# Toeplitz products in four column tiles, pooling bands built at the start, rows of y ahead of gate rows in a trunk kernel

## The chip, the cores and the metric

The kernel is one launch on one core of a Trainium2 chip. Its time is in device microseconds (us), taken from the start to the end of the program on that core; lower is better. A core has five engines that run their own instruction streams and wait for each other on semaphores: TensorE (PE in the profile; PEld is its weight load), VectorE (DVE), ScalarE (ACT), GpSimd (POOL) and SyncE (SP, which here only issues transfers). ScalarE issues some transfers too. Matmul results land in PSUM, 8 banks of 128 x 512 float32.

## The reference, cut to what matters

Two layers over 512 tokens of width 1024, float32. Each sub-layer is an RMS norm with shift, scale and gate made from a conditioning vector `c` (adaLN), a mixer or an MLP, and a gated residual. The change lies in the first mixer, `_ab_mixer`, and in the adaLN products beside it:

```python
def _modulate(x, c, g, w, b):
    m = (c @ w + b)[:, None, :]
    shift, scale, gate = jnp.split(m, 3, axis=-1)
    h = _rmsnorm(x, g) * (1.0 + scale) + shift
    return h, 1.0 + gate

def _ab_mixer(h, ...):
    proj = h @ w_in                         # 1024 -> 512 (ua) + 512 (ub)
    ya = _pool_mixer(ua, pool_w, pool_scale)  # trailing means over 2, 4, 8, 16 tokens, minus identity
    yb = _s5_mixer(ub, ...)                 # 32 groups of 16 channels, 64 complex states each
    return jnp.concatenate([ya, yb], axis=-1) @ w_out
# in _s5_mixer: y = Re(C h) + D u;  y = gelu(y);  y = y * sigmoid(y @ w_glu + b_glu)
```

## The kernel before

Every large product is done as three float32r products (high by high, high by low, low by high), so each weight slot of 1024 x 256 is loaded by SyncE into `w_raw`, rounded by ScalarE to `w_hi` (`prep` on ScalarE, L751) and subtracted by VectorE to `w_lo` (`prep` on VectorE, L1283). TensorE then makes two tiles of 128 x 512 a slot, 24 products each (`tile`, `first_tiles`). Two buffers of each kind alternate, so ScalarE may round slot n only when TensorE has finished slot n-2.

The order of each engine's instructions is written by hand; nothing schedules them. What stands around the change, in order of time:

- **Start.** VectorE computes the parameters of the SSM (`sm`, `pw_re`, `bz`, `f_re`, `f_im`). TensorE multiplies `c` with the first adaLN columns (`ada_pair`) and sums them to columns by products with ones (`ada_columns`, 128x1). `first_scales` on VectorE must be done before the second `ada_columns`, and `first_shifts` follows that. `modulate(0)` then gives `h_hi`, `h_lo`, and the input projection `AB_IN` (four slots) starts.
- **SSM.** TensorE transposes `f` to `e_re`, `e_im` (what a run of eight tokens puts into the states), multiplies the inputs with it (`injections`) and VectorE scans over the 64 runs in two halves (`chain`). The part inside a run is a Toeplitz matrix per group: its 16 x 128 first rows `kr` come from 32 products of `bd` (32 columns of weights) with `g_re` and `g_ni`, four `skip_d` products add the diagonal. ScalarE copies `kr` out of PSUM, and 16 transfers (8 of SyncE at L569, 8 of ScalarE at L873) shift it into `toep`. `half_outputs` multiplies `toep` with the inputs and adds the states' part, for 16 groups at a time.
- **Exchange of y.** ScalarE applies GELU into `y_run`. Eight transfers a half write it to memory by rows (L584 on SyncE, L890 on ScalarE), two read it back by channels into `y_t` (L588). ScalarE and VectorE split it into `yg_hi` and `yg_lo`, and TensorE makes the GLU product from these.
- **Pooling.** `v_tok` is the product of `ua` with the pooling weights, copied by ScalarE. The trailing means are products with four banded matrices, `band(g)` and `first_band(g)` (the first 16 columns), which `make_band` builds on VectorE from `steps_off`. TensorE waits for them with `bands`.
- **Gates.** The remaining adaLN columns are six units (2 to 7) of eight steps each. A step adds one block of 128 rows times its entry of `c` on VectorE (`ada_step`, L1108 for the first of a unit, L1111 for the others, 128x512 in units 2 and 3, 128x768 in 4 to 7). The rows come from memory: sixteen in `ada_mid`, then 32 through eight homes, three in `ada_ring` and five in `ada_more`, each refilled when its step is done (`more_ada`, L534). When a unit's eight steps are done, TensorE sums it to columns (`ada_sums`, products with ones, alternating between PSUM banks 6 and 7), and VectorE adds the bias (`ada_collect`, L1240). `ada_sums` of unit 3 waits until unit 2 is collected.
- **Output projection** `AB_OUT`, four slots. Between two tiles of each slot TensorE makes the `ada_sums` of one unit (4 to 7), and VectorE adds the gated residual (L1431). GpSimd adds up the squares of the new x (L675). The norm of the first MLP begins with TensorE's sums of `sumsq`.

## Time and profile before

| | |
|---|---|
| median of 3 runs | 1289.25 us (1288.05 to 1290.51) |
| profiled execution | 1290.38 us, span 1288.6 us |
| busy: TensorE, VectorE, ScalarE, GpSimd | 96%, 59%, 35%, 7% of the span |
| mean granted clock of TensorE | 0.984 |
| ScalarE rounds a weight slot (L751) | mean 1895 ns |
| VectorE's low half of a slot (L1283) | mean 2320 ns |
| VectorE's gated residual (L1431) | mean 750 ns |
| one product of 128x512, start to start, 24 in a tile | 0.23 us |

A busy share is a mean over stages. TensorE's idle time is short and lies in a few places, so the waits and the timeline tell more than the shares. The granted clock is a share of TensorE's full speed: 1.00 is 2.4 GHz and 0.50 is 1.2 GHz. A float32 product leaves two records in the trace, a float32r product leaves one, so "x32" of float32 products are 16 of them. A number such as 0.39 us for a product is its own latency; the next starts 0.23 us after it.

### The profile page before, as it was taken

The numbers are of one execution on the slowest core, as the hardware profiler recorded it, in microseconds if no ns is written. First come the engines' busy times: TensorE is split into PE (matmuls) and PEld (weight loads), VectorE is DVE, ScalarE is ACT, GpSimd is POOL, SyncE is SP. The second block draws the span as 40 slices with busy tenths as digits, with TensorE's granted clock in tenths as the row PEclk, the third lists the DMA queues.
The fourth block names the chain that finished last, engine by engine and source line by source line (L and its number), as shares of the span: only waits on it lengthen the run. The fifth ranks groups of instructions, "written<-read, shape, count | busy, mean of one in ns | idle before, by whom it ended". The sixth has DMA issues, their size and how long they took to land.

```text
span 1288.6 us, 16165 instructions
## 1 busy us (share of the span) xinstructions
PE 1241.1 (96%) x6192; PEld 1004.8 (78%) x6192; DVE 761.0 (59%) x1041; ACT 448.7 (35%) x611; POOL 94.8 (7%) x128
## 2 busy tenths in 40 slices
PE   6999599999999999999999998999999999999999
PEld 3788588788888888888779885567788888888887
DVE  7898777754654645655468957864643443443432
ACT  5442412421422312323443247862432231331321
POOL 0010012000000000051000001114100000000022
PEclk9999799999999999999999998999999999999999
DMA  9558755544445444431223220003143223223311
GB/s 322 187 116 261 244 192 197 172 160 154 146 168 171 171 163 131 171 112 58 83 70 122 82 89 1 1 1 98 33 131 98 76 98 92 92 98 98 98 65 65
DMA packets 132686, 157.40 MB, mean 122 GB/s; under 512 B 19784, under 2 KB 113152, under 8 KB 132608
## 3 DMA queue, kind: packets, MB, share of 16 engines
q1 hardware_dynamic: 125328, 153.82, 36.4%
q10 hardware_dynamic: 7312, 2.96, 1.1%
q8 instruction: 30, 0.49, 0.2%
q14 instruction: 16, 0.13, 0.0%
...
## 4 chain that ended last, share of the span: by engine, by line
PE 84%; DVE 9%; DMA 3%; ACT 2%; issue 1%; SPq 1%; ACTq 0%; POOL 0%; DVEq 0%
PE psum L1646 83%; PE psum L1650 2%; DVE ada_acc_b L1111 1%; DVE work L1294 1%; DMA ada_first<-in_ada_w 1%; DVE w_lo L1283 1%; DVE h_lo L1304 1%; DVE ada_acc L1111 1%; DMA raw_bn<-in_ssm_b_im 1%; DMA y_scratch<-y_run 1%; ACT pT L1034 1%; SPq L534 0%; DVE s_t L1082 0%; DVE rstd L1111 0%; DVE s_im L1082 0%
## 5 line engine op out<-in xcount | busy, mean ns | idle before, releaser
L1646 PE MATMUL psum<-h_hi,w_hi 128*128 128x512 f32 (+1 forms) x872 | 343.1, 393 | 3.4 <-DVE w_lo L1283 3.3
L1646 PE MATMUL psum<-h_lo,w_hi 128*128 128x512 f32 (+1 forms) x872 | 340.5, 390 | 0.0
L1646 PE MATMUL psum<-h_hi,w_lo 128*128 128x512 f32 (+1 forms) x872 | 340.4, 390 | 0.0
L751 ACT ACTIVATE w_hi<-w_raw 128x2048 fp32r<-128x2048 f32 x92 | 174.3, 1895 | 285.6 <-PE psum L1646 285.0
L1283 DVE TENSOR_TENSOR w_lo<-w_raw,w_hi 128x2048 fp32r<-128x2048 f32 x92 | 213.4, 2320 | 100.2 <-ACT w_hi L751 99.7
L1646 PE MATMUL psum<-a_hi,w_hi 128*128 128x512 f32 x512 | 202.4, 395 | 0.0
L1646 PE MATMUL psum<-a_hi,w_lo 128*128 128x512 f32 x512 | 202.2, 395 | 0.0
L1646 PE MATMUL psum<-a_lo,w_hi 128*128 128x512 f32 x512 | 202.1, 395 | 0.0
L1646 PEld LDWEIGHTS psum<-h_hi,w_hi 128*128 128x128 f32 (+1 forms) x872 | 164.0, 188 | 42.6 <-issue 7.2
L1646 PEld LDWEIGHTS psum<-h_hi,w_lo 128*128 128x128 f32 (+1 forms) x872 | 163.9, 188 | 35.0
L1646 PEld LDWEIGHTS psum<-h_lo,w_hi 128*128 128x128 f32 (+1 forms) x872 | 163.9, 188 | 33.8
L1431 DVE SCALAR_TENSOR_TENSOR xT<-psum,mods,xT 128x512 f32<-128x512 f32 x80 | 59.4, 750 | 187.6 <-PE psum L1646 187.5
L1477 DVE TENSOR_TENSOR work<-work 128x512 f32<-128x512 f32 x64 | 44.2, 691 | 127.4 <-ACT work L945 126.6
L1646 PEld LDWEIGHTS psum<-a_hi,w_lo 128*128 128x128 f32 x512 | 96.3, 188 | 23.0
L1646 PEld LDWEIGHTS psum<-a_lo,w_hi 128*128 128x128 f32 x512 | 96.3, 188 | 22.8
L1646 PEld LDWEIGHTS psum<-a_hi,w_hi 128*128 128x128 f32 x512 | 96.3, 188 | 22.7
L945 ACT ACTIVATE work<-psum 128x512 f32<-128x512 f32 x64 | 38.2, 598 | 212.3 <-PE psum L1646 212.3
L1467 DVE SCALAR_TENSOR_TENSOR ada_acc<-ada_l_ring,pb,ada_acc 128x768 f32<-128x768 f32 x56 | 60.0, 1072 | 1.1
L663 POOL TENSOR_TENSOR sumsq<-xT 128x512 f32<-128x512 f32 x3 | 3.1, 1041 | 682.2 <-DVE xT L1431 682.2
L1481 DVE TENSOR_TENSOR a_lo<-work,a_hi 128x512 fp32r<-128x512 f32 x64 | 44.3, 693 | 2.6
L948 ACT ACTIVATE a_hi<-work 128x512 fp32r<-128x512 f32 x64 | 40.5, 633 | 2.0
L1646 PE MATMUL psum<-w_hi,h_hi 128*128 128x256 f32 x128 | 36.4, 284 | 0.0
...
## 6 DMA issues: line engine op xcount, KB each, us to landing
...
```

The source lines that it names most:

```text
L751: act.activation(w_hi[n % 2][:, :, 0:w], raw[n % 2][:, :, 0:w], ACT.Copy).then_inc(hi_ready, 1)
L945: act.activation(work[t % 2][:, 0:L], bank[(t0 + t) % 4], ACT.Relu)\
L948: act.activation(a_hi[:, t, :], work[t % 2][:, 0:L], ACT.Square)\
L1034: act.activation(pT[:, 0:i + 1, i * P:(i + 1) * P], bank[n % 2][:, 0:(i + 1) * P].rearrange("p (j q) -> p j q", q=P), ACT.Copy).then_inc(t ...
L1111: ins = dve.scalar_tensor_tensor(out=acc[:, 0:w], in0=row, scalar=pb[:, k:k + 1], in1=acc[:, 0:w], op0=ALU.mult, op1=ALU.add)
L1283: dve.tensor_tensor(w_lo[n % 2][:, :, 0:w], raw[n % 2][:, :, 0:w], w_hi[n % 2][:, :, 0:w].bitcast(F32), SB).then_inc(lo_ready, 1)
L1431: dve.scalar_tensor_tensor(out=xT[:, k, :], in0=bank[t % 4], scalar=mods[:, a, 16 + k:17 + k], in1=xT[:, k, :], op0=M, op1=A).then_inc(dve ...
L1467: ins = dve.scalar_tensor_tensor(out=ada_acc[:, :], in0=src, scalar=pb[:, k:k + 1], in1=ada_acc[:, :], op0=M, op1=A)
L1477: dve.tensor_tensor(work[2][:, 0:L], work[t % 2][:, 0:L], work[t % 2][:, 0:L], M)\
L1481: dve.tensor_tensor(a_lo[:, t, :], work[2][:, 0:L], a_hi[:, t, :].bitcast(F32), SB)\
L1646: return nc.tensor.matmul(o, lhsT, rhs, start=start, stop=stop, **kw)
L1650: return nc.tensor.transpose(o, in_, ident[0:n, 0:n])
```

## The change

There are four parts.

1. **Toeplitz products.** `kr_part(q)` is quarter q of the partitions of PSUM bank 0. Groups t, t+1, t+2, t+3 go to the four quarters (four column tiles), where before all went to the first 32 partitions of banks 0 and 1 in turn. ScalarE copies quarters 0 and 1, VectorE quarters 2 and 3 inside `chain(0)`.
2. **Bands.** `make_band` runs at the start: band 0 before VectorE's wait for `setup_act`, bands 1 to 3 between `f_im` and `first_scales`. A band is five operations where it was seven, and it lies in `ada_acc`. GpSimd makes `steps_off` without waiting for `h_ready`.
3. **Transfers.** SyncE issues the second `w_out` slot and the first three gate rows behind the exchange of y.
4. **Gate steps and sums.** `ada_sums` of unit u waits for the collecting of unit u-2 (the last user of its bank) and not u-1. The steps are spread anew: 20 before the output projection where there were 25, and 28 in it.

```diff
--- before.py
+++ after.py
@@ -189,14 +189,14 @@
 
     def band(g):
 
-        return work[g // 2][:, g % 2 * (BAND + PAD):g % 2 * (BAND + PAD) + BAND]
+        return ada_acc[:, g * (BAND + PAD):g * (BAND + PAD) + BAND]
 
     def first_band(g):
 
-        return work[g // 2][:, g % 2 * (BAND + PAD) + BAND:(g % 2 + 1) * (BAND + PAD)]
-
-    steps_off = work[0][:, 2 * (BAND + PAD):2 * (BAND + PAD) + BAND]
-    band_tmp = work[1][:, 2 * (BAND + PAD):2 * (BAND + PAD) + BAND]
+        return ada_acc[:, g * (BAND + PAD) + BAND:(g + 1) * (BAND + PAD)]
+
+    steps_off = work[3][:, 0:BAND]
+    band_tmp = work[3][:, BAND:2 * BAND]
 
     at = [e_at]
     s_re = lay(at, "s_re", [P, GT, NRUN])
@@ -488,6 +488,9 @@
         return y_dram.rearrange("(g c) t -> c g t", c=C)[
             :, half * GT:(half + 1) * GT, i * NRUN:(i + 1) * NRUN]
 
+    def kr_part(q):
+        return bank[0][2 * C * q:2 * C * (q + 1), :]
+
     block = nc.Block()
     block.__enter__()
 
@@ -562,7 +565,7 @@
               .then_inc(u_in, 16)
         load(AB_OUT, slots[AB_OUT])
 
-        sp.wait_ge(mats_out, 12)
+        sp.wait_ge(kr_ready, 4)
         sp.wait_ge(toep_zero, 1)
         for m in range(1, RUN, 2):
             for g2 in range(2):
@@ -576,8 +579,6 @@
             sp.dma_start(ada_mid[:, 2 * j:2 * j + 2, :],
                          ada_w[0, a, j % 4 * 2 * P:(j % 4 + 1) * 2 * P, c0:c0 + w].rearrange("(r p) n -> p r n", p=P))\
               .then_inc(ada_mid_in[j], 16)
-        load(AB_OUT + 1, slots[AB_OUT + 1])
-        more_ada(3)
         for half in range(2):
             sp.wait_ge(y_copied, 2 * half + 2)
             for i in range(1, RUN, 2):
@@ -586,11 +587,13 @@
             sp.wait_ge(y_out_s[half], 16 * RUN)
             for ct in (2 * half, 2 * half + 1):
                 sp.dma_start(y_t[:, ct, :], y_dram[ct * P:(ct + 1) * P, :]).then_inc(y_in[half], 16)
-        more_ada(6)
+        more_ada(3)
+        load(AB_OUT + 1, slots[AB_OUT + 1])
+        more_ada(5)
         load(AB_OUT + 2, slots[AB_OUT + 2])
         more_ada(8)
         load(AB_OUT + 3, slots[AB_OUT + 3])
-        more_ada(15)
+        more_ada(16)
         assert ada_next[0] == 2 * ADA_STEPS - ADA_EARLY
         sp.wait_ge(cat_ready, 8)
 
@@ -645,7 +648,6 @@
         own(pool.iota(rot_c[:, 0, :].bitcast(I32), pattern=[[1, NRUN]], base=0, channel_multiplier=0))
         settle()
         pool.tensor_copy(run_no[:, :], rot_c[:, 0, :].bitcast(I32)).then_inc(consts, 1)
-        pool.wait_ge(h_ready, 8)
         own(pool.iota(band_tmp.bitcast(I32), pattern=[[1, BAND]], base=0, channel_multiplier=-1))
         settle()
         pool.tensor_copy(steps_off, band_tmp.bitcast(I32)).then_inc(steps_ready, 1)
@@ -861,12 +863,11 @@
         for r in range(2):
             copy_tile(first_tile[AB_IN + 2] + r, ua[:, r, :])
         prep(GLU)
-        for i in range(8, 12):
-            act.wait_ge(mats_ps, i + 1)
-            t = (i - 8) * 4
-            act.activation(kr[:, t:t + 4, :].rearrange("p t n -> p (t n)"), bank[i % 2][0:2 * C, :],
-                           ACT.Copy).then_inc(mats_out, 1)
-        act.wait_ge(mats_out, 12)
+        act.wait_ge(mats_ps, 9)
+        for q in range(2):
+            act.activation(kr[:, q::4, :], kr_part(q).rearrange("p (t n) -> p t n", n=P), ACT.Copy)\
+               .then_inc(kr_ready, 1)
+        act.wait_ge(kr_ready, 4)
         act.wait_ge(toep_zero, 1)
         for m in range(0, RUN, 2):
             for g2 in range(2):
@@ -1166,6 +1167,18 @@
         ts(v(K_), v(PH), magic, None, A)
         ts(v(K_), v(K_), -magic, None, A)
         tt(v(PH), v(PH), v(K_), SB)
+        def make_band(g):
+
+            win = float(WINDOWS[g])
+            ts(band_tmp, steps_off, 0.0, 1.0 / win, ALU.is_ge, M)
+            stt(band(g), steps_off, win, band_tmp, ALU.is_lt, M)
+            stt(band_tmp[:, 0:PAD], recip[:, :], 1.0 / win, band(g)[:, 0:PAD], ALU.max, M)
+            own(dve.scalar_tensor_tensor(out=first_band(g), in0=band_tmp[:, 0:PAD], scalar=win,
+                                         in1=ident[:, 0:PAD], op0=M, op1=SB))
+            tt(band(g)[:, 0:P], band(g)[:, 0:P], ident[:, :], SB)
+
+        dve.wait_ge(steps_ready, 1)
+        make_band(0)
         dve.wait_ge(setup_act, 5)
 
         tt(v(COS), v(SINH), v(SINH), M)
@@ -1287,6 +1300,9 @@
         tt(f_im[:, :, :, :], fb(bz[1]), fp(pw_re), M)
         tt(f_tmp_b[:, :, :, :], fb(bz[0]), fp(pw_im), M)
         dve.tensor_tensor(f_im[:, :, :, :], f_im[:, :, :, :], f_tmp_b[:, :, :, :], A).then_inc(f_ready, 1)
+        for g in range(1, 4):
+            make_band(g)
+        dve.sem_inc(bands, 1)
         first_scales()
 
         def scaled(a, k):
@@ -1359,6 +1375,11 @@
             tt(flat(s_im), xi, flat(rot_c), M)
             tt(flat(s_t2), xr, flat(rot_s), M)
             dve.sem_inc(inj_read, 1)
+            if half == 0:
+                dve.wait_ge(mats_ps, 9)
+                for q in range(2, 4):
+                    dve.tensor_copy(kr[:, q::4, :], kr_part(q).rearrange("p (t n) -> p t n", n=P))\
+                       .then_inc(kr_ready, 1)
             tt(flat(s_re), flat(s_re), flat(s_t1), A)
             tt(flat(s_im), flat(s_im), flat(s_t2), SB)
             dve.wait_ge(decay_ready, half + 1)
@@ -1375,20 +1396,6 @@
         dve.wait_ge(inj_ps, 1)
         for half in range(2):
             chain(half)
-        def make_band(g):
-
-            win = float(WINDOWS[g])
-            for t, w in ((band(g), BAND), (first_band(g), PAD)):
-                tmp = band_tmp[:, 0:w]
-                if w == BAND:
-                    ts(tmp, steps_off, 0.0, 1.0 / win, ALU.is_ge, M)
-                else:
-                    ts(tmp, recip[:, :], 1.0 / win, None, ALU.max)
-                    stt(tmp, steps_off[:, 0:w], 0.0, tmp, ALU.is_ge, M)
-                stt(t, steps_off[:, 0:w], win, tmp, ALU.is_lt, M)
-                same = min(w, P)
-                tt(t[:, 0:same], t[:, 0:same], ident[:, 0:same], SB)
-
         def gelu_low(ct):
             dve.wait_ge(gelu_hi, ct + 1)
             dve.tensor_tensor(yg_lo[:, ct, :], y_t[:, ct, :], yg_hi[:, ct, :].bitcast(F32), SB)\
@@ -1396,22 +1403,16 @@
 
         prep(GLU)
         ada_steps(8)
-        dve.wait_ge(steps_ready, 1)
-        for g in range(4):
-            make_band(g)
-        dve.sem_inc(bands, 1)
         prep(AB_OUT)
-        gelu_low(0)
-        gelu_low(1)
-        ada_steps(8)
-        gelu_low(2)
-        gelu_low(3)
-        ada_steps(2)
+        ada_steps(4)
+        for ct in range(4):
+            gelu_low(ct)
+        ada_steps(4)
         for g in range(4):
             dve.wait_ge(cat_hi, g + 1)
             dve.scalar_tensor_tensor(out=h_lo[:, g, :], in0=bank[4 + g], scalar=pb[:, 16 + g:17 + g],
                                      in1=h_hi[:, g, :].bitcast(F32), op0=M, op1=SB).then_inc(cat_ready, 1)
-        ada_steps(7)
+        ada_steps(4)
         for m in range(4):
             dve.wait_ge(act_drain, drains[first_tile[GLU] + m][1])
             dve.tensor_tensor(cat_f[:, m, :].rearrange("p (k j) -> p j k", j=RUN),
@@ -1434,7 +1435,7 @@
         for i in range(4):
             n = AB_OUT + i
             prep(n + 1)
-            ada_steps((4, 4, 4, 0)[i])
+            ada_steps((6, 4, 4, 3)[i])
             for r in range(2):
                 residual(first_tile[n] + r, 2 * i + r, 0)
                 if r == 0:
@@ -1704,7 +1705,7 @@
 
         def ada_sums(value, unit, q=None):
 
-            pe.wait_ge(mods_part, unit if q is not None else unit - (unit > 3))
+            pe.wait_ge(mods_part, unit if q is not None else max(2, unit - 1))
             pe.wait_ge(ada_used, value - ADA_EARLY)
             acc = ada_acc if q is not None else ada_sum_home(unit)
             o = bank[7] if q is not None else bank[7 - unit % 2]
@@ -1846,18 +1847,17 @@
         pe.wait_ge(g_ready, 1)
         pe.wait_ge(skip_ready, 1)
         pe.wait_ge(act_drain, drains[first_tile[AB_IN + 3] - 1][1])
-        for i in range(8, 12):
-            if i >= 10:
-                pe.wait_ge(mats_out, i - 1)
-            for r in range(4):
-                t = (i - 8) * 4 + r
-                o = bank[i % 2][0:2 * C, r * P:(r + 1) * P]
-                for n_, (b_, g_) in enumerate(((bd[0], g_re), (bd[1], g_ni))):
-                    mm(o, b_[:, t, :], g_[:, t, 0:RUN, :].rearrange("p m c -> p (m c)"), n_ == 0 and r == 0, False,
+        for t4 in range(GT // 4):
+            for b_, g_ in ((bd[0], g_re), (bd[1], g_ni)):
+                for q in range(4):
+                    t = 4 * t4 + q
+                    mm(kr_part(q)[:, t4 * P:(t4 + 1) * P], b_[:, t, :],
+                       g_[:, t, 0:RUN, :].rearrange("p m c -> p (m c)"), t4 == 0 and g_ is g_re, False,
                        skip_group_check=True)
-            t = (i - 8) * 4
-            mm(bank[i % 2][0:2 * C, :].rearrange("p (t n) -> p t n", n=P)[:, :, 0:C], ident[0:2 * C, 0:2 * C],
-               skip_d[:, t:t + 4, :], False, True, skip_group_check=True).then_inc(mats_ps, 1)
+        for q in range(4):
+            last = mm(kr_part(q).rearrange("p (t n) -> p t n", n=P)[:, :, 0:C],
+                      ident[0:2 * C, 0:2 * C], skip_d[:, q::4, :], False, True, skip_group_check=True)
+        last.then_inc(mats_ps, 1)
         slot_ready(AB_IN + 3)
         for r in range(2):
             tile(AB_IN + 3, first_tile[AB_IN + 3] + r, r)
```

VectorE at the start, before (`f_im` is the last SSM operand, `mods` the scales and shifts, `h_lo` the low half of the modulated input):

```order
L1082 TENSOR_TENSOR f_tmp_b<-bz_134,pw_im 128x2048
L1289 TENSOR_TENSOR f_im<-f_im,f_tmp_b 128x2048
L1222 TENSOR_TENSOR mods<-psum,pa 128x8
L1224 SCALAR_TENSOR_TENSOR mods<-mods,pa 128x8
L1230 TENSOR_TENSOR mods<-psum,pa 128x8
L1294 SCALAR_TENSOR_TENSOR work_69<-xT,mods,psum 128x512
L1294 SCALAR_TENSOR_TENSOR work_70<-xT,mods,psum 128x512
```

and now:

```order
L1083 TENSOR_TENSOR f_tmp_b<-bz_134,pw_im 128x2048
L1302 TENSOR_TENSOR f_im<-f_im,f_tmp_b 128x2048
L1087 TENSOR_SCALAR work_72<-work_72 128x144
L1091 SCALAR_TENSOR_TENSOR ada_acc<-work_72 128x144
L1091 SCALAR_TENSOR_TENSOR work_72<-recip,ada_acc 128x16
L1176 SCALAR_TENSOR_TENSOR ada_acc<-work_72,ident 128x16
L1083 TENSOR_TENSOR ada_acc<-ada_acc,ident 128x128
L1087 TENSOR_SCALAR work_72<-work_72 128x144
...
L1176 SCALAR_TENSOR_TENSOR ada_acc<-work_72,ident 128x16
L1083 TENSOR_TENSOR ada_acc<-ada_acc,ident 128x128
L1235 TENSOR_TENSOR mods<-psum,pa 128x8
L1237 SCALAR_TENSOR_TENSOR mods<-mods,pa 128x8
L1243 TENSOR_TENSOR mods<-psum,pa 128x8
```

Fifteen operations of three bands stand between `f_im` and the first `mods`.

SyncE behind the `toep` transfers, before:

```order
L569 DMA toep<-kr 16x16x128 x2
L576 DMA ada_mid<-in_ada_w 128x2x512 x8
L514 DMA w_raw_52<-in_ab_w_out 128x8x256
L534 DMA ada_ring<-in_ada_w 128x768 x3
L584 DMA y_scratch<-y_run 16x16x64 x4
L588 DMA y_t<-y_scratch 128x512 x2
L584 DMA y_scratch<-y_run 16x16x64 x4
L588 DMA y_t<-y_scratch 128x512 x2
L534 DMA ada_more<-in_ada_w 128x768 x5
```

and now:

```order
L572 DMA toep<-kr 16x16x128 x2
L579 DMA ada_mid<-in_ada_w 128x2x512 x8
L585 DMA y_scratch<-y_run 16x16x64 x4
L589 DMA y_t<-y_scratch 128x512 x2
L585 DMA y_scratch<-y_run 16x16x64 x4
L589 DMA y_t<-y_scratch 128x512 x2
L537 DMA ada_ring<-in_ada_w 128x768 x3
L517 DMA w_raw_52<-in_ab_w_out 128x8x256
L537 DMA ada_more<-in_ada_w 128x768 x5
```

The first `w_raw` load and three `ada_ring` rows moved from ahead of the first `y_scratch` write to behind the last `y_t` read.

VectorE from the second half of `cat` to the residual of the first output tile (`cat_f` is the gated y, `mods` a collected unit), before:

```order
L1417 TENSOR_TENSOR cat_f<-gate_t,y_t 128x8x64 x4
L1422 TENSOR_TENSOR h_lo<-cat_f,h_hi 128x512 x4
L1240 TENSOR_TENSOR mods<-psum,pa 128x4 x2
L1251 TENSOR_SCALAR mods<-mods 128x8
L1283 TENSOR_TENSOR w_lo_56<-w_raw_52,w_hi_54 128x2048
L1111 SCALAR_TENSOR_TENSOR ada_acc<-ada_ring,pb,ada_acc 128x768 x2
L1111 SCALAR_TENSOR_TENSOR ada_acc<-ada_more,pb,ada_acc 128x768 x2
L1431 SCALAR_TENSOR_TENSOR xT<-psum,mods,xT 128x512
L1240 TENSOR_TENSOR mods<-psum,pa 128x6
```

and now:

```order
L1418 TENSOR_TENSOR cat_f<-gate_t,y_t 128x8x64 x4
L1423 TENSOR_TENSOR h_lo<-cat_f,h_hi 128x512 x4
L1253 TENSOR_TENSOR mods<-psum,pa 128x4 x2
L1264 TENSOR_SCALAR mods<-mods 128x8
L1296 TENSOR_TENSOR w_lo_56<-w_raw_52,w_hi_54 128x2048
L1112 SCALAR_TENSOR_TENSOR ada_acc_b<-ada_more,pb,ada_acc_b 128x768 x4
L1109 TENSOR_SCALAR ada_acc<-ada_ring,pb 128x768
L1112 SCALAR_TENSOR_TENSOR ada_acc<-ada_ring,pb,ada_acc 128x768
L1432 SCALAR_TENSOR_TENSOR xT<-psum,mods,xT 128x512
L1253 TENSOR_TENSOR mods<-psum,pa 128x6
```

Before, all eight steps of the unit in `ada_acc_b` and one of the next stood ahead of `cat_f` (25 steps in all); now four of them do, and its fifth to eighth step come behind the weights of the second slot.

## Rows read from the trace of the kernel before

**Rows 1.** Waits of TensorE, whole span: in total us, times, longest us.
```profile
PE psum L1646 <- DVE mods L1240: 11.5, 1, 11.5
...
PE psum L1646 <- ACT v_tok L894: 2.2, 1, 2.2
...
PE psum L1646 <- DVE yg_lo L1394: 1.7, 1, 1.7
```
**Rows 2.** Waits of VectorE, whole span.
```profile
DVE sm L1082 <- ACT sm L760: 1.3, 1, 1.3
```
**Rows 3.** Timeline, 38 to 44 us: start us, busy us, engine, line.
```profile
38.80 0.16 DVE L1222 TENSOR_TENSOR mods<-psum,pa 128x8 f32<-128x8 f32 x1
...
41.16 1.98 PE L1646 MATMUL psum<-ones,first_acc 128*128 128x1 f32 x16 [0.19 <-ACT first_acc L776]
...
43.18 0.17 DVE L1230 TENSOR_TENSOR mods<-psum,pa 128x8 f32<-128x8 f32 x1 [4.03 <-PE psum L1646]
```
**Rows 4.** Windows, with busy times, granted clock, DMA share, GB/s.
```profile
42.00:46.00 4.00, 4.00 (x24) 4.00 (x25) 2.41 (x5) 1.34 (x2) 0.00 (x0) 0.62 0.94 268
...
107.00:126.00 19.00, 17.90 (x219) 17.44 (x218) 16.89 (x39) 5.28 (x9) 0.00 (x0) 1.00 1.06 370
...
127.00:133.00 6.00, 5.86 (x36) 5.89 (x37) 0.41 (x1) 1.07 (x2) 0.00 (x0) 0.72 0.48 137
```
**Rows 5.** Timeline of VectorE, the first band.
```profile
116.22 0.23 DVE L1086 TENSOR_SCALAR work<-work 128x144 f32<-128x144 f32 x1
116.48 0.31 DVE L1090 SCALAR_TENSOR_TENSOR work<-work,work 128x144 f32<-128x144 f32 x1
116.83 0.29 DVE L1082 TENSOR_TENSOR work<-work,ident 128x128 f32<-128x128 f32 x1
117.15 0.17 DVE L1086 TENSOR_SCALAR work<-recip 128x16 f32<-128x16 f32 x1
```
**Rows 6.** Timeline of TensorE: adaLN products, and `kr` products, first and last.
```profile
21.80 7.09 PE L1646 MATMUL psum<-ada_first,c_wide 128*64 128x512 f32 x32 [1.05 <-ACT xT L765]
...
85.79 0.41 PE L1646 MATMUL psum<-g_re,bd 128*32 128x128 f32 x2
...
93.92 0.29 PE L1646 MATMUL psum<-skip_d,ident 32*32 32x64 f32 x2
```
**Rows 7.** Timelines of VectorE and ScalarE, 88 to 95 us.
```profile
88.14 0.69 DVE L1082 TENSOR_TENSOR s_t<-psum,rot_s 128x512 f32<-128x512 f32 x1
...
94.25 0.59 ACT L867 ACTIVATE kr<-psum 32x512 f32<-32x512 f32 x1 [1.50 <-PE psum L1646]
94.87 7.00 ACTq L873 DMA_DIRECT2D toep<-kr  x8
```
**Rows 8.** Timeline of TensorE at four places.
```profile
106.19 3.79 PE L1646 MATMUL psum<-u_run,toep 128*128 128x64 f32 x32 [0.87 <-DMA toep<-kr]
...
133.43 0.47 PE L1646 MATMUL psum<-yg_hi,w_hi 128*128 128x512 f32 x1
...
146.63 0.95 PE L1646 MATMUL psum<-ones,sumsq 128*128 128x1 f32 x8
...
213.67 0.95 PE L1646 MATMUL psum<-ones,sumsq 128*128 128x1 f32 x8
```
**Rows 9.** Timeline of SyncE's DMA queue.
```profile
105.36 4.27 SPq L576 DMA_DIRECT2D ada_mid<-in_ada_w  x8
```
**Rows 10.** Timeline of VectorE between 146 and 164 us.
```profile
146.82 5.50 DVE L1111 SCALAR_TENSOR_TENSOR ada_acc_b<-ada_more,pb,ada_acc_b 128x768 f32<-128x768 f32 x5
...
152.78 3.87 DVE L1417 TENSOR_TENSOR cat_f<-gate_t,y_t 128x512 f32<-128x512 f32 x4
...
161.39 2.29 DVE L1283 TENSOR_TENSOR w_lo<-w_raw,w_hi 128x2048 fp32r<-128x2048 f32 x1
```
**Rows 11.** Critical chain, 200 to 206 us, and GpSimd's timeline there.
```profile
202.50 1.88 DVE ada_acc L1111
...
201.81 1.74 POOL L675 TENSOR_TENSOR sumsq<-sumsq,work 128x512 f32<-128x512 f32 x1 [5.19 <-ACT work L921]
```

## The prediction

> **What bounds the kernel now.** I read the engines' waits first. TensorE is busy for nearly all of the span, so a gain can only come out of the few places where it idles or repeats work; its three longest waits in the part that the change touches are 11.5 us for `mods` on VectorE, 2.2 us for `v_tok` on ScalarE and 1.7 us for `yg_lo` [rows 1]. All lie between 85 us and 160 us. Then I read the timelines of the engines there, to see what ends each wait, and last the stretch from 160 us to 213.67 us, where TensorE starts the row sums of the next norm [rows 8]. After that point both programs have the same instructions in the same order, so the change of the time is the change of that one instant. The reader is to see that four chains meet on the way to it: the first adaLN scales, the Toeplitz part of the SSM, the exchange of y through memory, and VectorE's gate steps.
>
> **First stretch: the bands in front of the first scales.** Band 0 (five small operations) goes where VectorE waits 1.3 us for ScalarE anyway [rows 2]. Bands 1 to 3 go between `f_im` and the first scales. One band costs 0.26 + 0.35 us for the two 128x144 operations, 0.32 us for the 128x128 one (the distances between their starts) and twice about 0.19 us for the two of 16 columns: 1.3 us [rows 5]; three cost 3.9 us. The first scales now start at 38.80 us and take 0.36 us with the operation after them; VectorE then stood 4.03 us waiting for TensorE until 43.18 us [rows 3]. TensorE's column sums, which wait for these scales, began at 41.16. With the bands the scales are ready at 38.8 + 3.9 + 0.4 = 43.1, so the sums, the shifts and all of the input projection come 1.9 us later. Nothing hides that: TensorE works without a gap from there to 85.8. And the granted clock was already 0.62 in 42 to 46 us [rows 4], that is 1.2 GHz most of the time, after a stretch of one-column sums; 1.9 us more of idle time in front lets it stay there into the projection. I take 0.7 us for that, between 0 and 1.7. Stretch: +2.6 us (1.9 to 3.6).
>
> **Toeplitz products.** Before: 32 products and four products for the skip diagonal, from 85.79 to about 94.1 us [rows 6]. Two records (one product) take 0.22 us, so the 32 take 7.0 us and the skip products with their changes of tile the other 1.3 us. All write the same 32 output partitions. In four column tiles, four products can run side by side. What rows show of that: the adaLN products of the start write two halves of the partitions in turn, and 16 products of 512 columns take 7.09 us, 0.44 us each [rows 6]; a float32 product of 128 columns alone takes 0.22 us, so one of 512 would need 0.87. Two column tiles do run side by side. Four are not in the trace; the bounds are 7.0 us (no overlap) and 7.0/4 = 1.75 us, and since two overlap in full I take 1.75, plus 0.3 for the skip products: 2.05 us, 6.2 us less.
> For four tiles beside each other the Trainium skill is more careful: "TensorE: Matmul & The Clock Gate", Part 3, measured 2.38 times for three column tiles; by that share of the ideal the 32 products would take about 2.2 us, an estimate, and the sum would be 0.5 us worse.
> TensorE is not what the Toeplitz matrix waits for, though. It waits for `kr` in SBUF and the 16 transfers behind it. Before, the last copy of `kr` starts at 94.25, the transfers at 94.87 [rows 7] and TensorE starts on `toep` at 106.19 after 0.87 us of idling [rows 8], 11.3 us after the transfers began. Now the products end at 85.79 + 2.05 = 87.85. ScalarE copies two quarters (0.59 us each, as the row of 94.25) until 89.1; VectorE copies the other two, but only behind the four products of its chain, the last of which starts at 88.14 and takes 0.69 [rows 7]: 88.8 + 2 x 0.65 = 90.2. The transfers start there, 4.7 us earlier, and `toep` is whole at 101.5. TensorE has meanwhile done its two projection tiles (11.1 us) by 99.0 and waits 2.5 us instead of 0.87.
> The skill has the rule for this: "TensorEngine Tiling (Array Packing)", PSUM Bottleneck, says that tiling speeds up TensorE and not the evacuation of PSUM. The sum above agrees: of 6.2 us saved on TensorE, 4.7 reach the transfers.
> The wait of 2.5 us has a price of its own. After the 2.2 us wait for `v_tok` the granted clock of 127 to 133 us was 0.72 [rows 1, 4], so TensorE ran at 1.2 GHz for 6 x 0.28/0.5 = 3.4 us and lost 1.7 us of work. I book 1.7 us here too (0 to 1.7). The two copies also push VectorE's chain by 1.3 us; its second half is needed only 11 us after `toep` lands, so that is hidden. Stretch: -4.7 + 1.7 = -3.0; with the first stretch, -0.4. The two halves of y, the pool products, the copies of `v_tok` and the band products keep their order and length (106.19 to 133.43 [rows 8]): the GLU starts at 133.0.
>
> **Rows of y, and the gate rows behind them.** SP now writes y's rows before it fetches the next `w_out` slot and three gate rows. The eight `ada_mid` transfers (4.2 MB, issued in 4.3 us from 105.36 [rows 9]) still lie ahead of them. At the 370 GB/s of 107 to 126 us [rows 4] these need 11.3 us; they start near 101.6 now and are through by 115, so the rows meet a queue that is almost empty. The last half of y is back at about 130 instead of 136.6, and its low parts are ready at about 132, before the GLU starts. The wait of 1.7 us for `yg_lo` goes. The moved `w_out` slot arrives near 136 and is first wanted by ScalarE's cast at 147: hidden. GLU: 133.43 to 146.63 before [rows 8], less 1.7, so it ends at 133.0 + 11.5 = 144.5.
>
> **Gate sums.** The two sums behind the GLU no longer wait for VectorE's collecting of the first, so the 11.5 us wait for `mods` goes, and TensorE works on the first half of the output projection while VectorE makes the second half of `cat`. That looks like the largest gain, and most of it isn't one, because VectorE sets the pace there. VectorE starts `cat_f` at 152.78 before, after seven gate steps [rows 10]. Now the sigmoids set it: the first GLU tile ends about 2 us before the last, so `cat_f` starts at 143.3, and with the same 6.2 us of `cat` and 0.5 us of collecting VectorE is free at 150.0 instead of 161.39 [rows 10], 11.4 us earlier. But it has 28 gate steps before it, not 23: 20 are done, against 25. A step costs 1.08 us (five in 5.4 us, row of 146.82), a first one of eight 0.6, a low half of weights 2.2 [rows 10], a residual 0.66, one of TensorE's sums 1.35, a tile 5.5, ScalarE's cast 1.9 (the page's durations, less where the next operation overlaps). And where GpSimd adds squares, a step costs 0.9 us more: the critical chain has one of 1.88 us at 202.50, while GpSimd works from 201.81 for 1.74 us [rows 11]; I count one after each residual from the second on. By these, VectorE goes: weights to 152.2, six steps 158.1, residual, three steps 162.2, residual and weights 165.1, and the three steps that the second sum (inside the second slot) needs end at 169.2. TensorE has finished that slot's first tile at 164.3 and waits 4.9 us. From there a round is sum 1.35, tile 5.5, cast 1.9, weights 2.2, three steps 3.2 and a collision 0.9: 15.1 us, in which TensorE has 12.4 us of work. Sums at 169.2, 184.3, 199.3; then sum and last tile, 206.2. The same walk through the order of before gives 213.1 where the trace has 213.67, so I add 0.6: 206.8, 6.9 us earlier than before. Each of the three waits (4.9, 2.7, 2.7 us, each followed by one-column sums) can drop the clock as at 127 us, for up to 1.7 us, and here the tile behind it is on the chain.
>
> **Sum.** Behind the front there are four places where the clock can fall; I book three, the one before `toep` among them, two here: 206.8 + 3.4 = 210.2. That is 3.5 us before 213.67. The profiled execution took 1290.38 us for its span of 1288.6, 1.1 us over the median of the three runs: 1286.9 against it, 1285.8 against the median of 1289.25.
>
> **Rivals.** (a) The clock holds: none of the waits drops it, and the front costs 1.9. Then 206.8 - 1.7 - 0.7 = 204.4, 9.3 us gained, 1280.0. For it: the sum near 206 had 1 us of idling before it and kept the clock. Against: the one wait of over 2 us in dense work lost it. (b) All four are lost and the front costs 3.6: 212.9, a gain of 0.8, 1288.5: no change. (c) The four column tiles run one after the other. `kr` is then ready at about 94.4, and `toep` lands 4.2 us later than forecast: a loss of 0.7, 1290.0, no change. Against it: the two tiles of the start. (d) Slower: `ada_mid`'s transfers start when the projection is done, 11.1 us after the products end, and `toep`'s own traffic ends about 12.5 us after them. If the big transfers get ahead of the last small ones, `toep` waits for up to 4.2 MB at 370 GB/s, 11.3 us less the 2.9 that it would have waited: 8.4 us, 4.9 slower than before, 1294.1. It decides from the point where `toep` lands over 4 us after the tiles' end. Against it: an issue needs over 1 us to become traffic, and by then little is left.
>
> **Chances.** Forecast 0.48, (a) 0.20, (b) 0.20, (c) 0.06, (d) 0.06. A change under 0.2% (2.6 us) can't be told from none. Forecast splits: with two to three losses it is faster (0.37), with a fourth it is not (0.11). Faster 0.57, same 0.37, slower 0.06. The range 1280 to 1290 takes in (a) to (c); (d) and the edges are left out.
>
> **What would show it.** Column sums of the start near 43.1; `kr` products in 2 to 2.3 us and `kr` transfers 2 us earlier than 94.87 in all (4.7 less 2.6); a wait of about 2.5 us before `toep` and a granted clock of 0.5 behind it; no wait inside the GLU; then three waits of TensorE for gate steps of 5, 3 and 3 us where there was one of 1. I am wrong if TensorE does not wait there, if `toep` lands over 4 us after the tiles, or if anything after the first norm of the MLP changes its length.

## The result, and the profile after

| | before | after |
|---|---|---|
| median | 1289.7 us (4 runs) | 1304.5 us (4 runs, 1303.7 to 1306.7) |
| ratio, 95% interval | | 1.0119 (1.0102 to 1.0137) |
| profiled execution, span | 1288.6 us | 1302.0 us |
| mean granted clock | 0.984 | 0.974 |

The change made the kernel slower by 14.8 us; the forecast was 1285.8, with 1280 to 1290 as its range. All of the loss lies where the prediction looked: TensorE starts the row sums of the next norm at 227.02 us instead of 213.67 [rows 8], 13.35 us later, and the span is 13.4 us longer. Behind that point both traces take the same 1075 us.

TensorE's waits in the kernel after (in total us, times, longest us):

```profile
PE psum L1647 <- DVE ada_acc L1112: 9.8, 2, 5.3
...
PE psum L1647 <- DVE ada_acc_b L1112: 3.3, 1, 3.3
PE psum L1647 <- DMA toep<-kr: 2.8, 1, 2.8
...
PE psum L1647 <- ACT v_tok L895: 2.2, 1, 2.2
PE psum L1647 <- DVE mods L1237: 2.1, 1, 2.1
```

The 11.5 us for the gate rows' `mods` and the 1.7 us for `yg_lo` are gone [rows 1]. In their place stand 2.1 us for the first scales, 2.8 us for `toep` and 13.1 us for gate steps. The new waits are 18.0 us, less 0.9 and 1.05 us that were there before; the old ones were 13.2. The sum of the waits is 3 us worse, and the kernel 13 us. So the waits alone can't be the loss. TensorE's timeline at the places of [rows 3, 8]:

```profile
42.79 3.54 PE L1647 MATMUL psum<-ones,first_acc 128*128 128x1 f32 x16 [2.15 <-DVE mods L1237]
...
105.06 4.86 PE L1647 MATMUL psum<-u_run,toep 128*128 128x64 f32 x32 [2.81 <-DMA toep<-kr]
...
116.87 7.09 PE L1647 MATMUL psum<-u_run,toep 128*128 128x64 f32 x32
...
130.91 5.70 PE L1647 MATMUL psum<-pool_w_t,ua 128*128 128x128 f32 x32
...
143.49 0.48 PE L1647 MATMUL psum<-yg_hi,w_hi 128*128 128x512 f32 x1
...
154.74 0.95 PE L1647 MATMUL psum<-ones,sumsq 128*128 128x1 f32 x8
...
179.71 2.69 PE L1647 MATMUL psum<-ones,ada_acc 128*128 128x1 f32 x12 [5.28 <-DVE ada_acc L1112]
...
198.44 1.54 PE L1647 MATMUL psum<-ones,ada_acc_b 128*128 128x1 f32 x12 [3.25 <-DVE ada_acc_b L1112]
...
217.04 2.69 PE L1647 MATMUL psum<-ones,ada_acc 128*128 128x1 f32 x12 [4.53 <-DVE ada_acc L1112]
...
227.02 0.95 PE L1647 MATMUL psum<-ones,sumsq 128*128 128x1 f32 x8
```

The 32 `toep` products of a half took 3.79 us before and take 7.09 now, with nothing idle between them. `toep` starts 1.1 us earlier than before and the GLU 10.1 us later. The windows say why (us; busy us of PE, PEld, DVE, ACT and POOL with their instructions; granted clock; DMA share; GB/s):

```profile
104.00:108.00 4.00, 2.94 (x24) 2.94 (x25) 3.78 (x5) 1.97 (x2) 0.00 (x0) 0.94 0.88 283
108.00:112.00 4.00, 4.00 (x29) 3.88 (x31) 3.86 (x7) 0.00 (x0) 0.00 (x0) 0.50 1.02 381
...
128.00:132.00 4.00, 4.00 (x33) 3.88 (x34) 0.00 (x0) 0.99 (x2) 0.00 (x0) 0.50 0.00 0
132.00:136.00 4.00, 4.00 (x25) 4.00 (x25) 0.00 (x0) 0.10 (x1) 0.00 (x0) 0.64 0.57 131
...
180.00:184.00 4.00, 4.00 (x16) 3.71 (x16) 2.21 (x5) 0.63 (x1) 1.27 (x1) 0.50 0.86 303
184.00:188.00 4.00, 4.00 (x14) 3.14 (x14) 2.73 (x3) 0.00 (x0) 0.00 (x0) 0.74 0.72 224
```

About 2.5 us behind the end of the 2.8 us wait, at 107.5, the clock falls to 0.50, 1.2 GHz, and stays there for some 27 us; before, it was 1.00 in the whole stretch [rows 4]. The busy share shows nothing of this: TensorE reads 4.00 of 4 us at either clock. Behind the wait of 5.3 us it is low again, from 180 to about 186 us.

The kernel before had a long low clock too, at another place: from 148.7 to 165.8 us, through its 11.5 us wait for `mods` and on into the output projection.

```profile
159.09 1.87 PE L1646 MATMUL psum<-ones,rstd 128*128 128x1 f32 x8 [11.51 <-DVE mods L1240]
```

```profile
160.00:164.00 4.00, 4.00 (x13) 3.32 (x14) 2.94 (x4) 0.00 (x0) 0.00 (x0) 0.50 0.00 0
164.00:168.00 4.00, 4.00 (x15) 3.22 (x14) 3.67 (x4) 0.00 (x0) 0.00 (x0) 0.77 0.80 262
```

From these sums to the next ones TensorE needed 15.1 us before (159.09 to 174.17) and 11.9 us after (155.55 to 167.44), so the change also brought 3.2 us of clock here.

### The profile page after: what moved, and what is told of

Read it like the earlier page. It is cut to its first block, busy times and chain, and to the rows that moved or that the text cites. A ratio compares the mean times of both kernels' runs of the same rounds, so it can differ in the third digit from the quotient of the medians.

```text
span 1302.0 us, 16158 instructions
## 1 busy us (share of the span) xinstructions
PE 1252.2 (96%) x6192; PEld 1015.9 (78%) x6192; DVE 761.4 (58%) x1035; ACT 447.0 (34%) x609; POOL 94.4 (7%) x128
## 4 chain that ended last, share of the span: by engine, by line
PE 86%; DVE 7%; DMA 3%; ACT 2%; issue 1%; SPq 1%; POOL 0%; DVEq 0%; ACTq 0%
PE psum L1647 85%; DMA w_raw<-in_ab_w_in 2%; DVE work L1310 1%; PE psum L1651 1%; DVE h_lo L1320 1%; DVE ada_acc L1112 1%; DVE w_lo L1296 1%; ACT w_hi L753 1%; DMA w_raw<-in_mlp_w 1%; DVE ada_acc_b L1112 1%; ACT pT L1035 1%; SPq L572 0%; DMA toep<-kr 0%; DVE cat_f L1418 0%; ACT h_hi L800 0%
## 6 DMA issues: line engine op xcount, KB each, us to landing
ada_first<-in_ada_w SPq DMA_DIRECT2D x5, 1024.0 KB, 15.1
```

## The experiments

Each was timed against the kernel before, on one chip with it, the first four in three rounds and the others in five. Times are medians; the table is a summary, and the reasoning stands below it.

| kernel | us | executions | ratio to before (95%) |
|---|---|---|---|
| after + 3 fillers | 1290.1 | 10 | 0.9986 (0.9948 to 1.0024) |
| after, bands later | 1300.1 | 10 | 1.0051 (1.0024 to 1.0079) |
| after, `kr` as before | 1303.1 | 10 | 1.0054 (1.0015 to 1.0093) |
| after, gates as before | 1298.7 | 10 | 1.0035 (1.0006 to 1.0064) |
| before + 2 fillers | 1289.4 | 12 | 0.9989 (0.9965 to 1.0014) |
| after + 6 products behind the wait | 1298.3 | 12 | 1.0041 (1.0016 to 1.0065) |
| after + 4 fillers, bands later | 1287.9 | 12 | 0.9973 (0.9947 to 0.9999) |
| the same + new gate spread | 1269.4 | 6 | 0.9815 (0.9776 to 0.9855) |
| the same, 1 filler, `kr` as before | 1273.0 | 6 | 0.9870 (0.9834 to 0.9907) |
| after + new gate spread alone | 1283.6 | 12 | 0.9947 (0.9917 to 0.9976) |
| before + 2 fillers, new sum wait | 1280.0 | 8 | 0.9910 (0.9876 to 0.9943) |

The kernel before had medians of 1291.6, 1290.2 and 1289.9 us in the three series. The ratios compare means; the first series, with the first four kernels, has more of the kernel's longer executions (below), and so its ratios lie lower than the medians suggest. The kernel after was timed in a series of its own, with 1289.7 us for the kernel before, so a difference to its 1304.5 us compares two series.

One more thing holds for all differences below. Behind the norm's sums all kernels have the same instructions, yet in the profiled executions that part took between 1070.4 and 1075.0 us. It took 1075.0 in the kernel after, whose clock fell there at 602, 790 and 930 us, and 1070.4 with three fillers, where it fell only at 776. So up to 4.6 us of a difference can come from behind the change, and where it matters I give the instant of the norm's sums too (227.02 in the kernel after).

**Fill the wait before `toep`.** Products of the identity with 512 columns of `u_run`, into a bank that nobody reads. Their results are not used.

```diff
+        pe.wait_ge(kr_ready, 4)
+        for _ in range(3):
+            mm(bank[1], ident[:, :], u_run[:, 0:8, :].rearrange("p g k -> p (g k)"), True, True)
         pe.wait_ge(toep_in, 16 * 2 * RUN)
```

> The changed kernel with three filler products (identity by 512 float32 columns, 0.87 us each, into a PSUM bank that is free then) in TensorE's 2.8 us wait for toep; nothing else. Theory (clock): that wait drops the clock to 1.2 GHz, and the y products behind it (64-column products, each with its own weight load) are not enough to raise it again, so they run from 107 to 134 us at half speed; with the wait filled they take the 18.7 us of before instead of 31.6 us. The GLU ends 9 to 12 us earlier and the time falls by 8 to 12 us, to 1293 to 1297. Rival (gate steps): VectorE's gate steps in the output projection set the end, and the y products are slow beside them; then the time falls by under 3 us, to 1302 or more. Rival (the slow y products have another cause, such as the transfers running beside them): the granted clock stays at 0.5 there and the time is unchanged, 1304 to 1306.

Measured: 1290.1 us, under the 1293 to 1297 that I had expected; nine of ten executions between 1287.7 and 1293.2, the tenth at 1305.0 with a mean clock of 0.972. Adding work that nobody needs made the kernel 14.4 us faster. The timeline of its profiled execution:

```profile
102.06 2.73 PE L1647 MATMUL psum<-u_run,ident 128*128 128x512 f32 x6
...
105.68 3.79 PE L1647 MATMUL psum<-u_run,toep 128*128 128x64 f32 x32 [0.89 <-DMA toep<-kr]
...
144.14 0.95 PE L1647 MATMUL psum<-ones,sumsq 128*128 128x1 f32 x8
...
215.73 0.95 PE L1647 MATMUL psum<-ones,sumsq 128*128 128x1 f32 x8
```

```profile
108.00:112.00 4.00, 4.00 (x60) 3.93 (x60) 3.86 (x7) 0.00 (x0) 0.00 (x0) 1.00 1.03 386
```

`toep` starts no earlier (105.68 against 105.06), but the clock is 1.00 behind it, its half takes 3.79 us again, and from there to the end of the pool products it is 18.7 us, as before. The sums at the GLU's end start at 144.14 instead of 154.74. The transfers beside the products are as dense as in the kernel after (386 GB/s in this window, 381 there), so the loss in this stretch is the clock and nothing else. At the norm's sums 11.3 us are won; the other 4.6 us between the two profiled executions lie behind them.

**Bands 1 to 3 behind the first scales**, as the only edit to the kernel after.

> The changed kernel with bands 1 to 3 built behind the first scales and not in front of them, where VectorE waited 4.0 us for TensorE in the kernel before. Theory: the 3.2 us by which the input projection starts later (49.5 against 46.3 us) come back in whole, for the 3.6 us of bands fit into that wait; all later steps move up by as much: 1301 to 1302, 3 us less. Rival (the start does not matter, since transfers or the phase of the clock decide later): under 1 us. The long low clock behind toep stays in either case.

Measured: 1300.1 us (1296.4 to 1305.4), 4.4 under the kernel after. In the profiled execution the column sums of the start begin at 41.44 us (after: 42.79; before: 41.16) and the projection at 46.30 (49.50; 46.31), so what the forecast charged for the front comes back. But it is spent again: the wait for `toep` grew to 3.72 us, the clock was low from 101 to 136 us and once more from 139 to 146, and the norm's sums came 3.4 us later than in the kernel after:

```profile
230.44 0.95 PE L1647 MATMUL psum<-ones,sumsq 128*128 128x1 f32 x8
```

This execution, of 1302.6 us, is shorter than the kernel after only behind that point, where its clock fell less often. That the 4.4 us of the medians come from the front is not shown.

**The Toeplitz products as before**, one after the other on 32 partitions, with ScalarE's four copies.

> The changed kernel with the Toeplitz products of before: all in one column tile, banks 0 and 1 in turn, copied by ScalarE alone. TensorE has 6.2 us more of work. Theory (clock): the wait for toep shrinks from 2.8 us to 0.9 us, as before, so the clock stays at 1.00 through the y products. Toep lands about 4 us later than in the changed kernel, the y products take 12.9 us less: 8 to 9 us faster than the changed kernel, 1295 to 1297. Rival (tiles are a gain and the loss lies elsewhere): about 4 us slower than the changed kernel, 1308.

Measured: 1303.1 us, against 1295 to 1297 expected. Four of ten executions lie between 1292.6 and 1297.9, with a mean clock of 0.982 or more, and six between 1302.0 and 1308.7, with 0.979 or less. The profiled one, of 1306.6 us, is worth reading:

```profile
110.51 4.75 PE L1643 MATMUL psum<-u_run,toep 128*128 128x64 f32 x32 [1.01 <-DMA toep<-kr]
...
122.21 7.09 PE L1643 MATMUL psum<-u_run,toep 128*128 128x64 f32 x32
```

A wait of 1.01 us is enough here to lose the clock, where 0.87 us [rows 8] and 0.89 us (the kernel with fillers) did not. So the price is not steady: a wait of about 1 us before `toep` lost the clock in this trace and not in two others, while waits of 2.1 to 3.7 us there lost it in all five traces that have one.

**Does this happen to the kernel before too?** In the first series 13 of its 31 executions took 1297.3 to 1298.7 us, each with a mean clock of 0.976, and 17 took 1286.2 to 1292.0 with 0.984 or more (the one left took 1353.0 with 0.880 and is in no ratio). The edit: two of the same products before its wait for `toep`.

> The kernel before, with two products of 128x512 (0.45 us each) issued by TensorE between its two projection tiles and the wait for `toep`; nothing waits for them. Of 31 executions of the kernel before in the last series, about half took 1286.2 to 1292.0 us with a mean granted clock of 0.984 to 0.991, the rest 1297.3 to 1298.7 with 0.976. Theory: the longer ones are those in which the 0.87 us wait before `toep` already drops the clock to 1.2 GHz for the y products. Then with the wait filled none is left near 1298, and all executions lie at 1286 to 1291. Rival: the two levels have another cause, a drop elsewhere; then the share near 1298 stays at about half, and the median at 1291 or above.

Measured: ten of twelve at 1286.5 to 1291.5; two at 1294.7 and 1295.7 with a clock of 0.980; none at 0.976. Of the 29 executions of the kernel before in this series, six had 0.976 or less (1297.7 to 1299.1). If the filler did nothing, about two or three of twelve would be expected there, so none is a hint and no proof; and no trace of such an execution was taken. That the longer times of the kernel before come from its own 0.87 us wait is plausible, not shown.

**Heavy products behind the wait.** Six products of 512 columns, after `toep` has come, so that the wait itself stays.

```diff
+        pe.wait_ge(kr_ready, 4)
         pe.wait_ge(toep_in, 16 * 2 * RUN)
+        for _ in range(6):
+            mm(bank[1], ident[:, :], u_run[:, 0:8, :].rearrange("p g k -> p (g k)"), True, True)
```

> The changed kernel with six products of 128x512 directly behind the wait for `toep` (they don't fill the wait; the wait of 2.8 us stays). Theory: the wait drops the clock, and the y products, each of 64 columns with its own weights, can't raise it, while dense products of 512 columns can. Then the granted clock is back at 2.4 GHz by the time the y products start or shortly behind: the six cost 2.7 to 5.4 us, the y products take 19 us instead of 31.6, and the time is 1304.5 - 12.9 + 4 = 1295.6 (1293 to 1298). Rival: once dropped it stays low here for a fixed time whatever TensorE does: six slow products of 5.4 us on top, 1304.5 + 3 to 5 = 1308 to 1310.

Measured: 1298.3 us, 6.2 under the kernel after (4.2 at the norm's sums), though TensorE does 8 us more of useless work. Timeline and windows:

```profile
104.95 8.19 PE L1647 MATMUL psum<-u_run,ident 128*128 128x512 f32 x12 [3.59 <-DMA toep<-kr]
112.98 3.68 PE L1647 MATMUL psum<-u_run,toep 128*128 128x64 f32 x32
```

```profile
104.00:108.00 4.00, 3.05 (x4) 1.51 (x5) 3.90 (x6) 1.10 (x1) 0.00 (x0) 0.50 0.86 297
108.00:112.00 4.00, 4.00 (x7) 1.58 (x6) 3.90 (x7) 0.00 (x0) 0.00 (x0) 0.67 1.03 392
112.00:116.00 4.00, 4.00 (x31) 3.40 (x30) 3.69 (x5) 0.00 (x0) 0.00 (x0) 1.00 0.87 327
```

The wait drops the clock, and dense products raise it again while they run, 5.7 us after their start; the y products, 64 columns each behind a weight load of its own, then keep it at 1.00. In the kernel after the same y products did not raise it between 107.5 and 130.9 us. In all five traces with the clock low there, it came back only in the pool products of 128 columns, 2.4 to 4.6 us behind their start. That is what makes this wait so dear: the wait sets off the drop, and the light work behind it makes it last. My sum was 2.7 us short; the six products alone took 8.2 us where I had allowed 4 (2.7 to 5.4).

**The gate steps.** First the old spread and the old wait of the sums, in the kernel after (the four `ada_steps` counts and the sums' line as before).

> The changed kernel with the gate steps spread as before (25 ahead of the output projection, 23 in it) and with the sums of a unit waiting for the unit before it; tiles, bands and the order of the transfers as in the changed kernel. Theory: TensorE idles about 11 us for the first collecting again, but the output projection shrinks from 70.6 us to about 54 us; the two nearly cancel and the end of the projection moves by -4 to +1 us: 1300 to 1305. Rival (the new spread is most of the loss, 17.7 us in that stretch): 1290 to 1295.

Measured: 1298.7 us, between my two expectations and 5.8 under the kernel after (4.0 at the norm's sums), although the wait for `mods` is back (10.05 us in the trace). The two edits of the gates, taken together, cost more than they bring. Which of the two? With the fillers and late bands in place, only the spread was changed, from 20 steps in front of the gated product to 23, four of them now between the low parts of y:

```diff
-        for ct in range(4):
-            gelu_low(ct)
+        gelu_low(0)
+        gelu_low(1)
         ada_steps(4)
+        gelu_low(2)
+        gelu_low(3)
...
-        ada_steps(4)
+        ada_steps(7)
...
-            ada_steps((6, 4, 4, 3)[i])
+            ada_steps((6, 4, 4, 0)[i])
```

The kernel without this edit, fillers and late bands alone:

> The changed kernel with four filler products of 128x512 before the wait for `toep`, and with bands 1 to 3 built behind the first scales. Theory: with the clock kept, the 3 us that the bands cost in front come back in full: the median is that of the three-filler kernel (1290.1) less 2.7, 1287.4 (1286 to 1289). Rival: VectorE's 3.9 us of bands then delay `toep`'s copies and its chain, the wait grows past what four fillers cover (3.7 us was seen without fillers), and the clock drops in some or all executions: 1296 to 1300.

Measured: 1287.9 us, 2.2 under the kernel with three fillers, as expected; but that is another series, and there is one filler more. And with it:

> As the kernel with four fillers and late bands, and besides with four gate steps of VectorE between the low parts of y's two halves, where it idled 3.3 us, seven steps instead of four in front of the gated product, and none instead of three in the last round of the output projection. Theory: the output projection is paced by VectorE, so 3.3 us of steps done in its idle time come off the end, and the waits of 5.5, 3.3 and 3.3 us for the gate rows shrink: 1284 (1282 to 1286), 3 us under the kernel without this edit. Rival: the seven steps in front of the gated product wait for their rows, which SP fetches only behind the y exchange, and delay it: no gain or up to 3 us of loss, 1287 to 1291.

Measured: 1269.4 us, 18.5 less in the same series. I had expected 3, for three steps done in idle time. It is the best kernel of the study, 1.9% under the kernel before. The size made me look again at where the steps stand. TensorE's sum number k of the output projection needs 8(k+2) gate steps, so the second needs the 32nd. With 20 in front and 6 and 3 behind, 29 are done in the first round, and the 32nd stands in the second, behind the low half of the next slot's weights (`w_lo`). That waits for ScalarE's cast, and the cast for the slot's second tile, which TensorE runs only behind its sum. In the kernel after the sum starts at 179.71, the cast at the end of that tile, `w_lo` at 191.80, the three steps at 194.01 and the next sum at 198.44:

```profile
189.85 1.92 ACT L753 ACTIVATE w_hi<-w_raw 128x2048 fp32r<-128x2048 f32 x1 [8.43 <-PE psum L1647]
```

Each round is then one chain through three engines, and these steps do not overlap. With 23 (or 25, as before) the 32nd is done in the first round, ahead of `w_lo`. To test this apart from the clock and the bands, the new spread alone in the kernel after:

> The changed kernel with the spread of gate steps of the last kernel (four of them between the low parts of y's halves, seven in front of the gated product, none in the last round) and nothing else: no fillers, bands early. Theory: the output projection's rounds of 18.7 us come from the 32nd gate step standing behind the low half of the next slot's weights, which itself waits for a tile of TensorE; with 23 steps in front of the gated product the 32nd comes before it, as in the kernel before with 25, and a round takes TensorE's 13 us. The clock's drop before `toep` stays. So 1304.5 - 18.5 = 1286 (1283 to 1290). Rival: the 18.5 us were only to be had with the clock kept; with the wait before `toep` the y rows come back so late that VectorE has no idle time filled by it, and the gain is that of the three steps, 3 to 6 us: 1298 to 1301.

Measured: 1283.6 us, as expected (1283 to 1290), 20.9 less than the kernel after and 17.9 earlier at the norm's sums. The wait before `toep` is still there and the clock is 0.50 behind it, and the round has changed:

```profile
174.94 1.39 PE L1649 MATMUL psum<-ones,ada_acc 128*128 128x1 f32 x12
...
188.23 1.67 PE L1649 MATMUL psum<-ones,ada_acc_b 128*128 128x1 f32 x12 [0.85 <-DVE ada_acc_b L1112]
...
202.22 1.47 PE L1649 MATMUL psum<-ones,ada_acc 128*128 128x1 f32 x12
...
209.11 0.95 PE L1649 MATMUL psum<-ones,sumsq 128*128 128x1 f32 x8
```

Rounds of 13.3 and 14.0 us against 18.7 and 18.6, waits of none, 0.85 and none against 5.3, 3.3 and 4.5. Part of the gain is clock: it is low once in these rounds (189 to 193), three times in the kernel after. The four steps between the low parts of y were not tested apart, but the gain does not come from there: VectorE is free for the second slot's `w_lo` at 162.27, against 160.38. VectorE's windows agree. In the kernel after both engines have holes in a round (the second window begins with the sums that end the wait); with the new spread VectorE is the busy one and TensorE hardly idles. First after, then the new spread:

```profile
172.00:180.00 8.00, 2.72 (x13) 2.01 (x11) 7.79 (x7) 0.63 (x1) 2.57 (x1) 0.95 1.00 373
180.00:188.00 8.00, 8.00 (x29) 6.85 (x29) 4.95 (x7) 0.63 (x1) 1.27 (x1) 0.62 0.79 263
188.00:196.00 8.00, 7.19 (x32) 5.63 (x30) 4.95 (x3) 2.44 (x2) 2.87 (x1) 1.00 0.22 85
```

```profile
172.00:180.00 8.00, 8.00 (x43) 6.81 (x42) 7.65 (x7) 2.27 (x2) 2.60 (x1) 1.00 0.93 350
180.00:188.00 8.00, 7.37 (x33) 5.78 (x31) 7.52 (x8) 2.44 (x2) 1.41 (x1) 1.00 0.84 263
188.00:196.00 8.00, 7.77 (x33) 6.65 (x34) 7.69 (x8) 0.63 (x1) 2.60 (x1) 0.79 0.94 299
```

**What the other parts are worth.** The best kernel with the Toeplitz products as before:

> The best kernel so far (fillers, bands behind the first scales, new gate spread: 1269.4) with the Toeplitz products written as before, one after the other, with ScalarE's four copies, and one filler instead of four. Theory: what the four column tiles are worth is what reaches the `toep` transfers, 4.7 us of the 6.2 (less what VectorE's chain gives back): 1269.4 + 4.5 = 1274 (1272 to 1276). Rival: with one filler the wait drops the clock in some executions, as it did in the kernel with the old products: then part of them at 1280 to 1286.

Measured: 1273.0 us, 3.6 more, inside the expected 1272 to 1276. The two kernels were timed in different series with six executions each, and their intervals overlap (0.9776 to 0.9855, 0.9834 to 0.9907). That the four column tiles bring about what reaches the transfers, once nothing else eats it, agrees with this and is not shown by it. And the kernel before with two fillers and the relaxed wait of the gate sums, one line of the whole change:

```diff
-            pe.wait_ge(mods_part, unit if q is not None else unit - (unit > 3))
+            pe.wait_ge(mods_part, unit if q is not None else max(2, unit - 1))
```

> The kernel before with two edits: two fillers before the wait for `toep`, and the gate sums' wait per PSUM bank as in the change. It has the old spread (25 steps in front of the gated product), the old Toeplitz products, the late bands. Theory: the 11.5 us wait for `mods` goes, and no wait for gate steps of the kind of the changed kernel comes instead; VectorE sets the pace from the gated product on and gives back a part: 1289.4 - 8 = 1281 (1278 to 1284). Rival: VectorE's collecting and its steps merely move the wait to the next sums, as they did in the changed kernel: 1288 to 1292.

Measured: 1280.0 us, as expected (1278 to 1284), 9.4 under the kernel before with fillers alone. The wait for `mods` is gone, and so is the low clock behind it; 3.2 us of the wait came back as a wait for the second half of `cat`:

```profile
163.31 0.50 PE L1646 MATMUL psum<-h_hi,w_hi 128*128 128x512 f32 x1 [3.23 <-DVE h_lo L1422]
...
212.31 0.95 PE L1646 MATMUL psum<-ones,sumsq 128*128 128x1 f32 x8
```

Its 25 steps in front put the 32nd step into the first round, with the new wait of the sums, and the rounds' waits stay at 0.15, 1.19 and 1.54 us. That is a second trace for the reading above. The transfers of part 3 were never edited alone.

## Why the prediction was wrong

By its own steps, the forecast for the norm's sums was 210.2 us and the trace has 227.02: 16.8 us off, 10.2 at the end of the GLU (144.5 against 154.74) and 6.6 behind it.

- **Front, +2.6 (1.9 to 3.6): right.** The sums started at 42.79 for 43.1, took 3.54 us at the low clock for 1.98, and the projection came 3.2 us later.
- **Four column tiles, 2.05 us: right.** The products ran from 88.95 to about 91.05. Eight records now share one start interval of 0.22 us, where two did [rows 6]; the trace agrees with full overlap. The 2.2 us estimated from the Trainium skill ("TensorE: Matmul & The Clock Gate", Part 3) were too careful here: the 32 products took about 1.8 us.

```profile
88.95 0.43 PE L1647 MATMUL psum<-g_re,bd 128*32 128x128 f32 x8
89.19 0.40 PE L1647 MATMUL psum<-g_ni,bd 128*32 128x128 f32 x8
...
90.83 0.31 PE L1647 MATMUL psum<-skip_d,ident 32*32 32x64 f32 x8
```

- **Wait for `toep`, 2.5 us: right (2.81), also in that tiling speeds up TensorE and not the chain behind it.** VectorE's copies stood at 92.13 and the transfers began at 93.57; forecast with the front's 2.6 us: 92.8.
- **"The wait of 2.5 us has a price of its own ... I book 1.7 us here too (0 to 1.7)": this step failed.** From the start of `toep` to the end of the pool products the trace has 31.6 us, where 18.7 were needed before: 12.9 us, 11.2 more than booked. I had taken the price from the row behind `v_tok`, where the clock came back within 6 us [rows 4], and made it the upper end of the range. But the price of a drop is about half of the time that TensorE works until the clock is back (12.9 of 27.3 us here), and that depends on what follows. Fillers in the wait brought 11.3 us at the norm's sums, and heavy products behind it restored the clock: both show the mechanism. The kernel before already had a dearer drop than the one behind `v_tok`, the 3.2 us behind its wait for `mods`; the prediction did not read it.
- **y exchange ahead of the gate rows: right.** The wait for `yg_lo` is gone and the GLU takes 11.25 us (11.5 forecast). Being 10 us late, it starts at 143.49. The lateness is not the reason: with three fillers the GLU ends at 144.14, for 144.5 forecast, and has no such wait either, while the two kernels with the old order of transfers and fillers kept it (1.65 and 1.46 us).
- **Gate sums: the chain was right, the clock in it mis-sized.** From the GLU's end to the second sum I had 24.7 us, the trace 25.0. A round without the clock was 15.1; the trace has 18.7. Of the difference 3.2 us are the sums and the tile at the low clock (10.1 us from 179.71 to the tile's end, for 1.35 + 5.5), 0.4 the rest. I booked two losses of 1.7 us; there were three, of 3.2, 1.8 and 3.1, from the sums and tiles at 179.71, 198.44 and 217.04. These are 4.7 of the 6.6 us behind the GLU, and a late cast (next point) is 1.4. Even with the clock kept before `toep`, the kernel with three fillers needs 71.6 us from the GLU's end to the norm's sums, where I had 65.7. Here too the prediction took the loss behind `v_tok` as the most that a drop can cost.
- **Waits of TensorE for gate steps "of 5, 3 and 3 us": right**, 5.3, 3.3 and 4.5. The third is longer because ScalarE's last cast waited for the MLP's first weights, which SP fetched at 199.04 behind the gate rows; it began at 208.48, 1.4 us behind the end of the tile (VectorE's residual, 207.11). This I had not seen.

```profile
199.04 0.40 SPq L517 DMA_DIRECT2D w_raw<-in_mlp_w  x1
```

```profile
208.48 1.92 ACT L753 ACTIVATE w_hi<-w_raw 128x2048 fp32r<-128x2048 f32 x1 [8.33 <-DMA w_raw<-in_mlp_w]
```

- **The rivals.** (b), all clocks lost, had the right mechanism and stopped at 1288.5, since it multiplied the same 1.7 us. (a), (c) and (d) didn't occur; `toep` landed 11.5 us behind the start of its transfers, 11.3 before. No rival had a loss that grows with the light work behind it.
- **What the forecast walked past.** It worked out that a round has become a chain through three engines, 15.1 us with 12.4 of work for TensorE, and set it against the gain of the earlier start. It didn't ask which step of the spread makes the chain. It was three steps of VectorE, worth 17.9 us at the norm's sums, its share of the clock included: more than the 11.3 of the fillers.

Taken one by one from the kernel after (1304.5 us): fillers 14.4, new spread 20.9, late bands 4.4 alone and 2.2 with fillers. Together these would give 1267.0; the kernel that has all of them measured 1269.4. The 14.4 and the 20.9 each hold some 4.5 us from behind the norm's sums in the profiled executions, the bands' share is not shown, and the differences are between series, so the agreement is in part luck.
